# Hybrid attention and mixture-of-experts layer: the attention output is summed inside TensorE's back transposes and scaled by VectorE, and TensorE multiplies during its waits for the routing tables

## The chip, the cores and the metric

The kernel runs on one core of one Trainium2 chip. The metric is the device time of one execution in microseconds (us); less is better. The core's engines work side by side and wait for each other by semaphores: TensorE (PE, with its weight loads PEld), VectorE (DVE), ScalarE (ACT), GpSimd (POOL) and SyncE (SP, which issues most transfers).

## The reference

One layer on 1024 tokens plus 16 meta tokens, model width 1024, float32, batch 1:

```
h = h + hybrid_mixer(rmsnorm(h))   # two attention branches of 8 heads each, gated, one output projection
h = h + hier_moe(rmsnorm(h))       # top-1 of 4 groups, then top-2 of its 8 experts; 32 experts of width 256
out = rmsnorm(h)[:, 16:]

# attention, both branches, head width 64 (v) and chunk-causal mask:
p = softmax(s);  o = einsum('bhqk,bkhd->bqhd', p, v)
```

In branch A (dense heads) s is q times k with a rotary part; in branch B (sparse heads) only the 256 best keys of an indexer take part, with a bias by relative position. The experts' input rows are gathered by tables that are computed on the chip: for each token its two experts, its rank in each expert's list, and from these the slot of each token.

## The kernel before

One program goes through stages that are separated by blocks: input projection and indexer, threshold search, low-rank projections, attention, branch and output projections with the router, routing tables, 32 experts, final norm.

**Attention.** There are 16 heads, first 8 dense, then 8 sparse (HH = 16), and two super-steps s for each: an even (short) one over query blocks 0 to 3 with 5 key tiles, and an odd (long) one over query blocks 4, 5, 7, 6 with 9 key tiles. A super-step's softmax is computed per query block: TensorE makes the scores (`qk`), VectorE the row maximum (`row_max`; in sparse heads the score step that adds the bias and finds the maximum), ScalarE the exponential and its sum `den`; VectorE's reciprocal of `den` is `rec`. The order on TensorE is a list of turns, written out when the program is built. A "p" turn transposes one key tile of the probabilities (up to four 128x128 blocks) into a PSUM bank; ScalarE copies it as the rounded `pH`, VectorE writes the remainder `pL`, and three turns later TensorE multiplies both with the values (`pv`). Three PSUM banks rotate among the turns; `emptied(k)` is the wait until the reader of an earlier turn on the same bank is done. Because the values are split too (`VS` holds the rounded value in 64 columns and the remainder in the next 64), the output of a super-step is 128 rows for 64 channels: rows c and 64 + c have to be added.

For this there is one "q" turn per super-step, 32 in all. It is inserted at place 5 of the next super-step's turns, after ScalarE's copy `oT` of the output (L1329). TensorE transposes the four query blocks back to tokens (L1268), VectorE adds the two halves (`tensor_reduce` into `otmp`, L1389), and GpSimd multiplies by `rec` into `otok` (L1402, function `scaled`). Two heads share `otok`; an "o" turn, for every second head, transposes it (L1270), and ScalarE copies it to `OaT` or `ObT` (L1333). GpSimd's queue holds, per super-step, the split of the next head's values, queries and keys, then `scaled` of the super-step before, and at odd ones the issue of a bias join for a later head.

TensorE's operands are of two kinds: a tile declared F32R is multiplied in one pass as it is; the large products are therefore made of three such products of leading parts and remainders. Tiles declared F32 (as `ident`, `con`, `oT`, the router's `x2T` and `wr`) are multiplied as true fp32. `pe.transpose` uses the transpose mode.

**Around the branch projections.** After attention a block ends, semaphores are cleared, and the next block starts. There ScalarE (`rows_lead`) and VectorE (`rows_rest`) split the attention outputs, and TensorE's first product (L1578) waits for the first remainder.

**Routing tables** (`moe_tables`). VectorE runs a long chain of small steps. TensorE's part is `ranks`: it waits for `both` (s_rk), makes ranks (L1931, L1933) and totals (L1937), waits for the operands A and B (s_ab) and makes the slot products (L1942), waits again (s_ab) and makes the slots' weights (L1946). The slots give the tokens, by which GpSimd gathers the first expert's rows; then TensorE transposes them (L2238) and goes on with the experts.

Of the kernel before, what the change touches and what calls it, by code (L numbers as in the profile page):

```python
# [14 lines left out]
ALU = mybir.AluOpType  # L15
# [7 lines left out]
P = 128  # L23
# [65 lines left out]
def hybrid_layer(nc, a, out):  # L89

    ctx = ExitStack()
    with ctx:
# [63 lines left out]
        dmaskb = keep("dmaskb", 64, BF16)  # L156
        upperb = keep("upperb", P, BF16)
        onesb = keep("onesb", P, BF16)
        gcq = keep("gcq", 2)
        gckv = keep("gckv", 1)  # L160
        nhalf = keep("nhalf", 18)
# [194 lines left out]
        with block() as blk:  # L356
# [512 lines left out]
            def _(dve):  # L869
# [39 lines left out]
                dve.tensor_copy(dmaskb[:, :], con[:, K_DM:K_DM + 64]).then_inc(s_cb, 1)  # L909
                dve.tensor_copy(upperb[:, :], con[:, K_U:K_U + P]).then_inc(s_cb, 1)  # L910
                dve.memset(onesb[:, :], 1.0).then_inc(s_cb, 1)
                for n, (kind, p, t, part) in enumerate(idx_jobs):
                    bank = ps[:, 4 + n % 4, :]
                    dve.wait_ge(s_ie, 2 * (n + 1))
                    if kind == "q":
                        for u in range(2):
                            c, j = slice(512 * part, 512 * (part + 1)), 4 * p + 2 * t + u
                            lead = Qi2[64 * u:64 * (u + 1), j, c].bitcast(F32)
                            dve.tensor_tensor(Qi2[64 * (1 - u):64 * (2 - u), j, c],
                                              bank[64 * u:64 * (u + 1), :], lead, ALU.subtract).then_inc(s_il, 1)  # L920
                    else:
                        lo, hi = thirds[part]
                        for u in range(2):
                            dve.tensor_tensor(KiLo[64 * u:64 * (u + 1), lo:hi], bank[0:64, 0:hi - lo],
                                              KiHi[0:64, lo:hi].bitcast(F32), ALU.subtract).then_inc(s_il, 1)
# [121 lines left out]
        pH = [at(f"pH{k}", [P, 512], F32R, R_X + 4096 * k) for k in range(RING)]  # L1047
        pL = [at(f"pL{k}", [P, 512], F32R, R_X + 4096 * k + 2048) for k in range(RING)]
        oT = [at(f"oT{k}", [P, 512], F32, R_X + 4096 * RING + 2048 * k) for k in range(2)]
        otmp = [at(f"otmp{k}", [P, 4, VD], F32, R_S + 16384 + 1024 * k) for k in range(2)]  # L1050
        OaT = at("OaT", [P, 4, T], F32, R_W)
        ObT = at("ObT", [P, 4, T], F32, R_S)
        KR = [at(f"KR{k}", [P, L], F32, R_K + 4160 * k) for k in range(2)]
# [87 lines left out]
        def bank_of(k):  # L1141
            return ps[:, bank_no[k], :]

        (s_qk, s_ml, s_ex, s_t, s_ld, s_rs, s_pv, s_ot, s_qa, s_rc, s_om, s_oe, s_z, s_vz, s_hl, s_hr, s_vl,
         s_vr) = map(sem, ["s_qk", "s_ml", "s_ex", "s_t", "s_ld", "s_rs", "s_pv", "s_ot", "s_qa", "s_rc",
                           "s_om", "s_oe", "s_z", "s_vz", "s_hs", "s_hr", "s_vl", "s_vr"])

        with block() as blk:
# [51 lines left out]
            def _(pe):  # L1200
# [35 lines left out]
                def emptied(k):  # L1236
                    kind, s, _ = turns[k]
                    if kind == "p":
                        pe.wait_ge(s_rs, p_no[turns[k]] + 1)
                    elif kind == "q":  # L1240
                        pe.wait_ge(s_qa, s + 1)
                    else:
                        pe.wait_ge(s_oe, o_no[turns[k]] + 1)

                def turn(k):
# [17 lines left out]
                    for b in range(low(s, t) // P if kind == "p" else 0, 4):  # L1263
                        dst = bank[:, P * b:P * (b + 1)]
                        if kind == "p":
                            mm = pe.transpose(dst, px(s, 4 * (s % 2) + b)[:, P * t:P * (t + 1)], ident)  # L1266
                        elif kind == "q":
                            mm = pe.transpose(dst, oT[s % 2][:, P * b:P * (b + 1)], ident)  # L1268
                        else:
                            mm = pe.transpose(dst, otok[s % 2][:, P * b:P * (b + 1)], ident)  # L1270
                    mm.then_inc(s_t, 1)
# [66 lines left out]
            def _(dve):  # L1338
# [30 lines left out]
                for k in range(len(turns)):  # L1369
# [3 lines left out]
                    if kind == "p":  # L1373
                        if t == 0:
                            dve.wait_ge(s_ex, 4 * s + 4)
                            c = 4 * (s % 4)
                            if s >= 4:
                                dve.wait_ge(s_om, s - 3)
                            dve.reciprocal(rec[:, c:c + 4], den[:, c:c + 4]).then_inc(s_rc, 1)
                        n, lo = p_no[turns[k]], low(s, t)  # L1380
                        dve.wait_ge(s_ld, n + 1)
                        dve.tensor_tensor(pL[n % RING][:, lo:512], bank_of(k)[:, lo:512],  # L1382
                                          pH[n % RING][:, lo:512].bitcast(F32), ALU.subtract).then_inc(s_rs, 1)
                    elif kind == "q":
                        dve.wait_ge(s_t, k + 1)
                        if s >= 2:
                            dve.wait_ge(s_om, s - 1)
                        both = bank_of(k).rearrange("p (b l c) -> p b c l", b=4, l=2)
                        dve.tensor_reduce(otmp[s % 2][:, :, :], both, AX.X, ALU.add).then_inc(s_qa, 1)  # L1389
                    if k in qk_after and not opens(k):  # L1390
                        row_max(qk_after[k])

            @blk.gpsimd
            def _(pool):
                def scaled(s):
                    u, c = s // 2 % 2, 4 * (s % 4)
                    pool.wait_ge(s_qa, s + 1)
                    pool.wait_ge(s_rc, s + 1)
                    if s >= 4:
                        before = ("o", 4 * (s // 4) - 4 + 2 + s % 2, 0)  # L1400
                        pool.wait_ge(s_t, turn_of[before] + 1)
                    pool.tensor_tensor(otok[s % 2][:, :].rearrange("p (b c) -> p b c", b=4)[:, :, VD * u:VD * (u + 1)],  # L1402
                                       otmp[s % 2][:, :, :],
                                       rec[:, c:c + 4].unsqueeze(2).to_broadcast([P, 4, VD]),
                                       ALU.mult).then_inc(s_om, 1)

                def values(hh):
                    if hh >= 2:
                        pool.wait_ge(s_pv, p_no[last_tile(2 * (hh - 2) + 1)] + 1)
# [46 lines left out]
                for s in range(NSS):  # L1456
# [6 lines left out]
                            queries(hh + 1)  # L1463
                    elif hh + 1 < HH:
                        keys(hh + 1)
                    if s >= 1:
                        scaled(s - 1)
                    if s % 2 == 1 and s // 2 + 2 < H:
                        joined(pool, s // 2 + 2)
                scaled(NSS - 1)  # L1470

        with block() as blk:
            @blk.gpsimd
# [51 lines left out]
        with block() as blk:  # L1525
# [36 lines left out]
                        sp.dma_start(xn2_d[P * (b - 1):P * b, :], x2[(b - 1) % 2][:, :]).then_inc(s_xos[(b - 1) % 2], 16)  # L1562
            @blk.tensor
            def _(pe):
                for n in range(JOBS):
                    m, part = n // 2, n % 2
                    pe.wait_ge(s_bl, m + 1)
# [258 lines left out]
def moe_tables(nc, a, at, sem, block, ps, con, rl, upperb, onesb, R_H, R_K, wts, xn2_d, s_xos):  # L1826
# [88 lines left out]
    def gathers(pool):  # L1915
# [6 lines left out]
        for u in range(U):  # L1922
            pool.indirect_dma_start(out=xs[u][:, :], out_offset=None, in_=xn2_d,
                                    in_offset=bass.IndirectOffsetOnAxis(ap=tok_i[:, u:u + 1], axis=0),
                                    bounds_check=T - 1, oob_is_err=False).then_inc(wts["G"][u], 16)

    def ranks(pe):
        pe.wait_ge(s_rk, 1)
        for b in range(NB):
            for c in range(b):  # L1930
# [5 lines left out]
        for b in range(NB):  # L1936
            mm = pe.matmul(ps[:, 1, 0:NE], onesb[:, :], both[:, b, :], start=(b == 0), stop=(b == NB - 1))  # L1937
        mm.then_inc(s_rk, 1)
        for n in range(N2):
            if n % PART == 0:  # L1940
                pe.wait_ge(s_ab, 2 + n // PART)
            mm = pe.matmul(ps[:, 2, 0:NE], A[:, n, :], B[:, n, :], start=(n == 0), stop=(n == N2 - 1))  # L1942
        mm.then_inc(s_sl, 1)
        pe.wait_ge(s_ab, 2 + N2 // PART)
        for n in range(N2):
            mm = pe.matmul(ps[:, 3, 0:2 * NE], A[:, n, :], BW[:, n, :, :].rearrange("p c n -> p (c n)"),  # L1946
# [708 lines left out]
```

## Time and profile before

| | |
|---|---|
| median of 3 runs | 1461.71 us (1460.07 to 1461.95) |
| the profiled execution's own time | 1460.28 us |
| its span, first to last instruction | 1458.5 us |
| busy: PE / DVE / ACT / POOL | 1361.1 / 1007.6 / 659.6 / 459.2 us |
| attention stage | about 536 to 847 us |
| branch, output projections and router | 849 to 1054 us |
| routing tables (first transfer issue to first expert's transposes) | 1054.3 to 1077.9 us |

The profile is of one execution. A line of a timeline gives the start, the length, engine, line, what is written and read, the count of merged records, and in square brackets how long the engine was idle before it and what ended that. The lengths of matmul records overlap, since they are pipelined: what one costs TensorE is the distance from its start to the next one's start. PEclk is the share of TensorE's 2.4 GHz that was granted; 0.50 is its lower level, 1.2 GHz. A wait for several semaphores is put down to the one that came last by the profile.

### The profile page before, as it was taken

The page shows a single profiled execution, that of the slowest core. Times are in us where ns is not written, and L with a number is a line of the kernel's source. Part 1 is how long each engine was busy: PE and PEld are TensorE (multiplying, and loading weights), DVE is VectorE, ACT ScalarE, POOL GpSimd, SP SyncE. Part 2 cuts the span into 40 slices and gives each one's busy share as a digit, 9 for nine tenths or more (in the row PEclk, how much of TensorE's full clock was granted, in tenths as well). Part 3 has the DMA queues.
Part 4 walks back from the last instruction along what each step waited for, and adds up shares of the span by engine and source line. Part 5 has one row for each costly group of instructions (what it writes and reads, how often), then busy time and mean ns, then how long its engine had stood idle before and what let it go on. Part 6 is the DMA issues. An engine that isn't in the chain of part 4 may idle for free. (4 is left out here: it accounts for less than half of the span.)

```text
span 1458.5 us, 21714 instructions
## 1 busy us (share of the span) xinstructions
PE 1361.1 (93%) x7307; PEld 1117.2 (77%) x7308; DVE 1007.6 (69%) x1891; ACT 659.6 (45%) x1175; POOL 459.2 (31%) x497
## 2 busy tenths in 40 slices
PE   6989999999999999999999979999859999999973
PEld 4779888888989978888777768899857776777741
DVE  5448999999970277777777754342387777777746
ACT  5348323321212146777777741121135666666622
POOL 1100335421215545555555214200112332333313
PEclk9999999999999999999999989999959999999996
DMA  6031543257432904868776255222279999999818
GB/s 213 30 143 40 185 161 111 88 197 228 134 101 100 246 1 80 187 134 225 210 206 179 68 178 159 86 89 87 73 281 389 348 366 351 356 379 372 344 58 326
DMA packets 106926, 273.76 MB, mean 188 GB/s; under 512 B 27393, under 2 KB 56737, under 8 KB 94425
## 3 DMA queue, kind: packets, MB, share of 16 engines
q1 hardware_dynamic: 92208, 229.20, 45.5%
q0 software_dynamic: 13584, 38.62, 10.4%
q10 hardware_dynamic: 1048, 4.82, 0.9%
q8 instruction: 52, 0.85, 0.2%
q14 instruction: 34, 0.27, 0.1%
HBM read 246.99 MB, written 85.96 MB: 228 GB/s over the span
## 5 line engine op out<-in xcount | busy, mean ns | idle before, releaser
L445 PE MATMUL ps<-hHi,g_lead 128*128 128x512 f32 (+2 forms) x480 | 184.5, 384 | 5.8 <-DVE hLo L877 3.6
L330 DVE TENSOR_SCALAR_CACHE_REDUCE mask<-score,cand 128x272 bf16<-128x272 f32 (+6 forms) x224 | 185.5, 892 | 4.6 <-DVE cand L349 4.4
L2364 DVE TENSOR_TENSOR w_rest<-wgu,w_lead 128x1024 fp32r<-128x1024 f32 x128 | 156.0, 1222 | 46.4 <-ACT w_lead L2309 45.2
L446 PE MATMUL ps<-hLo,g_lead 128*128 128x512 f32 (+2 forms) x480 | 183.9, 383 | 0.0
L447 PE MATMUL ps<-hHi,g_rest 128*128 128x512 f32 (+2 forms) x480 | 182.6, 380 | 0.0
L1382 DVE TENSOR_TENSOR pL<-ps,pH 128x512 fp32r<-128x512 f32 (+3 forms) x224 | 124.8, 573 | 56.8 <-ACT pH L1321 54.2
L2309 ACT CAST w_lead<-wgu 128x1024 fp32r<-128x1024 f32 x124 | 130.8, 1055 | 48.3 <-PE ps L2252 48.3
L762 POOL TENSOR_TENSOR g_rest<-g_raw,g_lead 128x2048 fp32r<-128x2048 f32 x12 | 56.7, 4722 | 298.4 <-ACT g_lead L619 298.4
L1321 ACT CAST pH<-ps 128x512 fp32r<-128x512 f32 (+3 forms) x224 | 106.0, 495 | 53.8 <-PE ps L1266 53.1
L2250 PE MATMUL ps<-w_lead,x_lead 128*128 128x512 f32 x256 | 114.5, 447 | 4.0 <-DVE x_rest L2371 4.0
L2272 PE MATMUL ps<-wd,hmT 128*128 128x512 f32 x256 | 115.3, 593 | 1.6 <-DVE hmT L2387 1.0
L445 PEld LDWEIGHTS ps<-hHi,g_lead 128*128 128x128 f32 x480 | 90.9, 189 | 22.8 <-ACT relf L701 4.0
L447 PEld LDWEIGHTS ps<-hHi,g_rest 128*128 128x128 f32 x480 | 91.0, 190 | 16.7
L446 PEld LDWEIGHTS ps<-hLo,g_lead 128*128 128x128 f32 x480 | 90.8, 189 | 14.8
L2252 PE MATMUL ps<-w_lead,x_rest 128*128 128x512 f32 x256 | 102.0, 398 | 0.0
L2251 PE MATMUL ps<-w_rest,x_lead 128*128 128x512 f32 x256 | 101.1, 395 | 0.0
L2214 POOL DMA_INDIRECT ys_d<-ye,dk x32 | 32.2, 1007 | 216.5 <-DVE ye L2399 180.3
L1282 PE MATMUL ps<-pH,VS 128*128 128x512 f32 (+3 forms) x224 | 94.9, 424 | 0.9
L2272 PEld LDWEIGHTS ps<-wd,hmT 128*128 128x128 f32 x256 | 46.2, 190 | 47.8 <-issue 47.8
L1283 PE MATMUL ps<-pL,VS 128*128 128x512 f32 (+3 forms) x224 | 79.0, 353 | 0.0
L650 ACT ACTIVATE stage<-ps 128x512 f32<-128x512 f32 x32 | 19.1, 598 | 112.1 <-PE ps L447 112.0
L2250 PEld LDWEIGHTS ps<-w_lead,x_lead 128*128 128x128 f32 x256 | 49.2, 192 | 20.9 <-issue 7.2
(382 smaller groups left out, 3414.3 us busy)
## 6 DMA issues: line engine op xcount, KB each, us to landing
wgu<-in_w_exp_gate SPq DMA_DIRECT2D x32, 1024.0 KB
wgu<-in_w_exp_up SPq DMA_DIRECT2D x32, 1024.0 KB
wd<-in_w_exp_down SPq DMA_DIRECT2D x32, 1024.0 KB, 11.8
bias_d<-mask_d POOLq DMA_DIRECT2D x8, 2368.0 KB, 15.6
g_raw<-in_w_in SPq DMA_DIRECT2D x16, 1024.0 KB, 7.2
gates_d<-stage SPq DMA_DIRECT2D x32, 256.0 KB, 2.0
gt<-gates_d SPq DMA_DIRECT2D x32, 256.0 KB, 3.1
tbm<-bias_d SPq DMA_DIRECT2D x8, 976.0 KB, 6.2
```

The lines of the kernel that those rows point to most:

```text
L330: return dve.tensor_scalar(mask[:, OFF[i]:OFF[i + 1]], score[:, OFF[i]:OFF[i + 1]], thr, 0.0, op, ALU.add, accum_out=cnt[:, i:i + 1])
L445: pe.matmul(dst, x[0], y[0], start=(k == 0), stop=False)
L446: pe.matmul(dst, x[0], y[1], start=False, stop=False)
L447: return pe.matmul(dst, x[1], y[0], start=False, stop=(k == KT - 1))
L1321: act.copy(pH[n % RING][:, lo:512], bank_of(k)[:, lo:512]).then_inc(s_ld, 1)
L1382: dve.tensor_tensor(pL[n % RING][:, lo:512], bank_of(k)[:, lo:512], pH[n % RING][:, lo:512].bitcast(F32), ALU.subtract).then_inc(s_rs, 1)
L2250: pe.matmul(dst, xl[:, k, :], wl, start=(k == 0), stop=False)
L2251: pe.matmul(dst, xl[:, k, :], wr, start=False, stop=False)
L2252: mm = pe.matmul(dst, xr[:, k, :], wl, start=False, stop=(k == KT - 1))
L2272: mm = pe.matmul(ps[:, 5 + half, :], hmT[u % 2][:, k, :], wd[u][:, k, 512 * half:512 * (half + 1)], start=(k == 0), stop=(k == 1))
L2309: act.copy(w_lead[part][:, :, :, :], wgu[u][:, :, 2 * part:2 * part + 2, :]).then_inc(S["m_wl"], 1)
L2364: dve.tensor_tensor(w_rest[u][:, :, 2 * part:2 * part + 2, :], wgu[u][:, :, 2 * part:2 * part + 2, :], w_lead[part][:, :, :, :].bitcast(F3 ...
```

## The change

In attention the q turn no longer transposes with the identity. TensorE multiplies the same `oT` block with `fold`, a 128x64 tile of two identity matrices one above the other, which adds the halves while it transposes; the result has 64 columns per query block instead of 128. VectorE no longer reduces, it multiplies the four 64-column blocks by `rec` straight from PSUM into `otok`. GpSimd's `scaled`, the tile `otmp` and the semaphore s_qa are gone; the bank of a q turn is free when s_om has counted VectorE's multiplication. `fold` is built once by VectorE beside the other constants.

TensorE also gets fp32 products of a 128x128 with a 128x512 operand whose results are never read: two at the start of the block of the branch projections, three before its wait for `both` in the tables, two after the totals and one after the slot products.

```
+        fold = keep("fold", VD)
...
+                dve.tensor_tensor(fold[:, :], ident[:, 0:VD], ident[:, VD:2 * VD], ALU.add).then_inc(s_cb, 1)
...
-        otmp = [at(f"otmp{k}", [P, 4, VD], F32, R_S + 16384 + 1024 * k) for k in range(2)]
...
                     elif kind == "q":
-                        pe.wait_ge(s_qa, s + 1)
+                        pe.wait_ge(s_om, s + 1)
...
                         elif kind == "q":
-                            mm = pe.transpose(dst, oT[s % 2][:, P * b:P * (b + 1)], ident)
+                            mm = pe.matmul(bank[:, VD * b:VD * (b + 1)], oT[s % 2][:, P * b:P * (b + 1)], fold[:, :],
+                                           start=True, stop=True)
...
                     elif kind == "q":
                         dve.wait_ge(s_t, k + 1)
-                        if s >= 2:
-                            dve.wait_ge(s_om, s - 1)
-                        both = bank_of(k).rearrange("p (b l c) -> p b c l", b=4, l=2)
-                        dve.tensor_reduce(otmp[s % 2][:, :, :], both, AX.X, ALU.add).then_inc(s_qa, 1)
+                        dve.wait_ge(s_rc, s + 1)
+                        if s >= 4:
+                            dve.wait_ge(s_t, turn_of[("o", 4 * (s // 4) - 4 + 2 + s % 2, 0)] + 1)
+                        u, c = s // 2 % 2, 4 * (s % 4)
+                        dve.tensor_tensor(otok[s % 2][:, :].rearrange("p (b c) -> p b c", b=4)[:, :, VD * u:VD * (u + 1)],
+                                          bank_of(k)[:, 0:4 * VD].rearrange("p (b c) -> p b c", b=4),
+                                          rec[:, c:c + 4].unsqueeze(2).to_broadcast([P, 4, VD]),
+                                          ALU.mult).then_inc(s_om, 1)
...
-                def scaled(s):
-                    u, c = s // 2 % 2, 4 * (s % 4)
-                    pool.wait_ge(s_qa, s + 1)
-                    pool.wait_ge(s_rc, s + 1)
-                    if s >= 4:
-                        before = ("o", 4 * (s // 4) - 4 + 2 + s % 2, 0)
-                        pool.wait_ge(s_t, turn_of[before] + 1)
-                    pool.tensor_tensor(otok[s % 2][:, :].rearrange("p (b c) -> p b c", b=4)[:, :, VD * u:VD * (u + 1)],
-                                       otmp[s % 2][:, :, :],
-                                       rec[:, c:c + 4].unsqueeze(2).to_broadcast([P, 4, VD]),
-                                       ALU.mult).then_inc(s_om, 1)
...
             def _(pe):
+                for _ in range(2):
+                    pe.matmul(ps[:, 7, :], ident, con[:, 0:512], start=True, stop=True)
...
+    def awake(pe, turns):
+
+        for _ in range(turns):
+            pe.matmul(ps[:, 5, :], con[:, K_ID:K_ID + P], con[:, 0:512], start=True, stop=True)
+
     def ranks(pe):
+        awake(pe, 3)
         pe.wait_ge(s_rk, 1)
...
         mm.then_inc(s_rk, 1)
+        awake(pe, 2)
         for n in range(N2):
...
         mm.then_inc(s_sl, 1)
+        awake(pe, 1)
         pe.wait_ge(s_ab, 2 + N2 // PART)
```

## Rows read from the trace of the kernel before

**Rows 1.** Busy time (count) per engine, PEclk, DMA: dense head, sparse head, experts.
```profile
655.90:675.40 19.50, 19.20 (x138) 16.57 (x137) 14.20 (x27) 14.01 (x33) 11.15 (x12) 1.00 0.74 143
749.60:767.80 18.20, 17.11 (x113) 14.28 (x112) 14.90 (x36) 13.86 (x33) 10.29 (x11) 1.00 0.71 204
1110.00:1410.00 300.00, 298.44 (x1243) 211.83 (x1242) 228.85 (x326) 181.28 (x233) 91.52 (x114) 1.00 0.89 334
```

**Rows 2.** Timeline, dense head: row maximum after the reduction of a q turn.
```profile
656.87 0.71 DVE L1363 TENSOR_REDUCE negm<-ps 128x1 f32<-128x528 f32 x1 [0.24 <-PE ps L1233]
```

**Rows 3.** Timeline, sparse head: around a short and a long super-step's q turn.
```profile
742.89 0.33 PE L1266 MATMUL ps<-con,px 128*128 128x128 f32 x1 [0.59 <-DVE pL L1382]
...
749.57 0.68 DVE L1389 TENSOR_REDUCE otmp<-ps 128x256 f32<-128x512 f32 x1
...
750.90 0.74 ACT L1308 ACTIVATE px<-sbias,negm 128x528 f32<-128x528 f32 x1 [0.36 <-DVE negm L1359]
```

**Rows 4.** Timeline of TensorE, dense head: the two q turns and what follows.
```profile
654.99 0.60 PE L1268 MATMUL ps<-con,oT 128*128 128x128 f32 x4
655.35 0.48 PE L1282 MATMUL ps<-pH,VS 128*128 128x512 f32 x1
...
668.87 0.34 PE L1283 MATMUL ps<-pL,VS 128*128 128x384 f32 x1
669.32 0.65 PE L1266 MATMUL ps<-con,pxa 128*128 128x128 f32 x4
```

**Rows 5.** Timeline of TensorE, router: fp32 products of 36 columns.
```profile
1006.94 1.87 PE L1602 MATMUL ps<-wr,x2T 128*128 128x36 f32 x16
1008.65 0.47 PE L1617 MATMUL ps<-wo_lead,y_lead 128*128 128x512 f32 x1
```

**Rows 6.** Timeline of TensorE, final stage: fp32 products of 512 columns.
```profile
1426.72 2.07 PE L2590 MATMUL ps<-fa,con 128*128 128x512 f32 x2 [13.15 <-DMA fb<-ys_d]
1428.58 1.91 PE L2591 MATMUL ps<-fb,con 128*128 128x512 f32 x2
```

**Rows 7.** Groups by form, attention stage: reduction, its multiplication, a 256-column remainder.
```profile
L1389 DVE TENSOR_REDUCE otmp<-ps 128x256 f32<-128x512 f32 x32 | 21.9, 683 | 2.8 <-PE ps L1268 2.6
L1402 POOL TENSOR_TENSOR otok<-otmp,rec 128x256 f32<-128x256 f32 x32 | 19.6, 613 | 140.3 <-DVE otmp L1389 139.6
...
L1382 DVE TENSOR_TENSOR pL<-ps,pH 128x256 fp32r<-128x256 f32 x32 | 13.3, 417 | 0.5
```

**Rows 8.** Busy time and granted clock (PEclk) where it is low or rises.
```profile
539.80:546.40 6.60, 6.57 (x25) 5.95 (x26) 2.82 (x5) 2.75 (x7) 6.44 (x6) 0.50 0.00 0
852.60:857.00 4.40, 4.36 (x10) 3.47 (x11) 4.40 (x5) 4.40 (x6) 0.00 (x0) 0.50 0.85 255
857.00:861.00 4.00, 4.00 (x19) 3.24 (x18) 4.00 (x5) 1.64 (x2) 0.00 (x0) 1.00 1.05 401
1061.50:1067.70 6.20, 1.34 (x45) 1.23 (x45) 5.93 (x19) 4.21 (x6) 0.00 (x0) 0.50 1.00 423
1067.70:1085.60 17.90, 13.55 (x50) 12.01 (x51) 12.75 (x31) 2.21 (x3) 6.15 (x7) 0.50 0.61 226
1426.70:1430.50 3.80, 3.78 (x5) 1.72 (x6) 1.23 (x1) 0.72 (x2) 0.76 (x2) 0.50 1.02 417
```

**Rows 9.** Timeline, end of attention and start of the branch projections.
```profile
843.99 0.66 PE L1268 MATMUL ps<-con,oT 128*128 128x128 f32 x4 [0.21 <-ACT oT L1329]
...
845.46 0.61 POOL L1402 TENSOR_TENSOR otok<-otmp,rec 128x256 f32<-128x256 f32 x1 [4.38 <-DVE otmp L1389]
...
846.12 0.66 PE L1270 MATMUL ps<-con,otok 128*128 128x128 f32 x4 [1.47 <-POOL otok L1402]
...
852.64 0.77 PE L1578 MATMUL ps<-o_lead,wb_lead 128*128 128x512 f32 x1 [5.87 <-DVE o_rest L1696]
```

**Rows 10.** Timeline of TensorE, routing tables: slot products, weight products.
```profile
1067.70 3.60 PE L1942 MATMUL ps<-r_B,r_A 128*128 128x32 f32 x16 [4.86 <-DVE r_A L2060]
1074.25 1.06 PE L1946 MATMUL ps<-r_BW,r_A 128*128 128x64 f32 x4 [2.95 <-DVE r_BW L2083]
```

More of the change, by code:

```diff
@@ L1142, in bank_of @@
             return ps[:, bank_no[k], :]
-        (s_qk, s_ml, s_ex, s_t, s_ld, s_rs, s_pv, s_ot, s_qa, s_rc, s_om, s_oe, s_z, s_vz, s_hl, s_hr, s_vl,
-         s_vr) = map(sem, ["s_qk", "s_ml", "s_ex", "s_t", "s_ld", "s_rs", "s_pv", "s_ot", "s_qa", "s_rc",
+        (s_qk, s_ml, s_ex, s_t, s_ld, s_rs, s_pv, s_ot, s_rc, s_om, s_oe, s_z, s_vz, s_hl, s_hr, s_vl,
+         s_vr) = map(sem, ["s_qk", "s_ml", "s_ex", "s_t", "s_ld", "s_rs", "s_pv", "s_ot", "s_rc",
                            "s_om", "s_oe", "s_z", "s_vz", "s_hs", "s_hr", "s_vl", "s_vr"])
@@ L1465, in _ @@
                         keys(hh + 1)
-                    if s >= 1:
-                        scaled(s - 1)
                     if s % 2 == 1 and s // 2 + 2 < H:
                         joined(pool, s // 2 + 2)
-                scaled(NSS - 1)
         with block() as blk:
```

## The prediction

> **What bounds the kernel now.** I read the page first, then busy time by stage, the groups by form in the attention stage, TensorE's timeline in one head of either kind, the two places where its clock is low, and last the waits around the turn that changes. In both kinds of head TensorE is the fullest engine, but not equally [rows 1]: a dense head (two super-steps, 19.5 us) has it busy 19.20 us, a sparse head (18.2 us) 17.11 us, and there VectorE is busy 14.90 us. In the expert stage it is busy 298.44 of 300 us. So whatever the stages before the experts lose or win comes out at the end: nothing later waits for anything else.
>
> In a dense head TensorE goes from one product to the next with almost no gap, and after the turn of the change VectorE waits for TensorE: the row maximum that follows the reduction starts 0.24 us after it could, "<-PE" [rows 2]. In a sparse head it is mixed: TensorE waits 0.59 us for VectorE's remainder in the short super-step [rows 3], and in the long one ScalarE waits 0.36 us for VectorE's score step.
>
> **What a q turn costs TensorE.** There are 32 q turns. Before, one is 4 transposes of 128x128 in transpose mode, one record each. They start at 654.99 and the next product at 655.35 [rows 4]: 0.36 us, 0.09 each. After, it is 4 true fp32 products with 64 moving columns. The trace has no such product with 64 columns; the nearest is the router's fp32 product with 36 columns. Its 8 products of one block leave 16 records, so each is issued as two instructions, each with a weight load; they start at 1006.94 and the next line at 1008.65 [rows 5]: 1.71 us, 0.107 per instruction. A 64-column stream is shorter than that at full clock (each instruction of a 512-column fp32 product starts 0.93 us after the one before at half clock [rows 6], so 64 columns are about 0.12 at half and 0.06 at full), so the load sets the pace and 0.107 holds. The new turn is 8 x 0.107 = 0.86 us, and the difference +0.49 us. Bounds: if the pair cost one load, 4 x 0.107 = 0.43, so +0.07; above, 0.49 in every turn.
>
> By the Trainium skill, FP8 and Floating Point Precision, section TensorE Precision Notes, true FP32 takes 4 passes through the array; 4 x 64 columns at 2.4 GHz are 0.107 us a product, 0.43 us a turn and only 0.07 us more than before, if the passes alone set the price. The rows above, where 36 columns cost 0.21 us a product, speak against reading it so: by the rows it is 0.86.
>
> **What a q turn costs VectorE.** The reduction from 512 PSUM columns takes 683 ns; a VectorE product over 128x256 with one PSUM operand takes 417 ns [rows 7]. I take 417 for the multiplication by rec: 0.27 us less a turn, 32 x 0.27 = 8.5 us of VectorE. GpSimd loses 32 x 613 ns, and with them its waits for VectorE (139.6 us) [rows 7]. Behind that wait stood the values, the keys and the bias join of later heads; they start earlier. Nobody on the other engines waits for them by any long row, so I price this at 0. The new waits of VectorE are for rec, which its own queue wrote a super-step before, and for an o turn of the super-step before: both long done. The bank of a q turn is freed 0.49 - 0.27 = 0.22 us later; the three banks rotate, so the turn that needs it comes three turns later, and this is hidden. One more VectorE instruction of 64 columns builds fold, long before attention; it is under the 417 ns of the 256-column one, 0 where TensorE's projections cover it.
>
> **What of it comes out, turn by turn.**
> Dense, long super-step, 8 turns: TensorE runs on without a gap after 655.35, and VectorE waits for it. All of the 0.49 comes out and none of VectorE's 0.27: +3.9.
>
> Dense, short super-step, 7 turns: after the turn TensorE streams a 384-column product from 668.87 (0.17 us: 384 of 512 columns of the 0.21 to 0.23 us that a product of 512 takes at full clock [rows 8]) and then idles 0.28 until 669.32, when ScalarE's exponential is ready [rows 4]. That exponential does not wait for the q turn. 0.28 is absorbed, 0.21 comes out: +1.5.
>
> Sparse, short super-step, 8 turns: the gap before 742.89 [rows 3] swallows it: 0.
>
> Sparse, long super-step, 8 turns: VectorE reduces from 749.57 and then does the score step, for which the exponential at 750.90 waits 0.36 us. VectorE's saving brings the score step up to 0.27 forward; TensorE's 0.49 pushes back both the product that it reads and the next transposes, whose copy ScalarE must make before that exponential. The two nearly cancel. I take +0.1 a turn: +0.8. Bounds: VectorE's chain alone decides, 8 x -0.27 = -2.1; or TensorE's cost in all 16 sparse turns, 16 x 0.49 = +7.8.
>
> The tail, 1 turn: the whole chain is exposed. From the last q turn (843.99) to the last o turn (846.12) [rows 9] lie the turn, the reduction and GpSimd's multiplication, which with its hand-over takes 845.46 to 846.12 = 0.66. New: +0.49 - 0.27 - 0.66 = -0.4.
>
> Attention: 3.9 + 1.5 + 0 + 0.8 - 0.4 = +5.8 us.
>
> **The products nobody reads, before the branch projections.** TensorE idles 5.87 us before 852.64 [rows 9], and when it starts its granted clock is 0.50, the 1.2 GHz level; it is at 2.4 GHz from 857.0, after 4.4 us of uninterrupted products [rows 8]. Those 4.4 us hold 10 products, 0.44 us each, the next 4.0 us 19, 0.21 each. So a microsecond at the low clock loses about half of itself, here 2.2 us. The two new products are fp32 with 512 columns, two instructions each, 0.93 us an instruction at 1.2 GHz [rows 6]: 3.7 us. They can start when the block does; from the end of the last o turn, 846.12 + 0.6, a block's change takes some 2.3 us, so at about 849.05, and they end at 852.8, 0.1 us late. If the clock again rises 4.4 us after the first product, that is 853.5: 0.7 us of low clock remain, 0.4 us. The gain is 2.2 - 0.4 - 0.1 = 1.7; I take 1.6. Bounds: two other starts of this trace stayed low for 3.8 and 6.6 us of work [rows 8], which gives 2.0 and 0.6; with no earlier rise, -0.1. VectorE's remainders come every 1.2 us for 1.4 us of full-clock products, so they can follow.
>
> **Those around the tables.** Three before the choice: 5.6 us at 1.2 GHz, from 1054.3, so over before the ranks start at 1061.5. Two after the totals, behind 1.34 us of rank products from 1061.5 [rows 8]: 3.7 us, over at 1066.6, 1.1 us before the slot products may start at 1067.70. One after those (1071.3): 1.9 us, over at 1073.2, before 1074.25 [rows 10]. So they delay nothing; cover left is 1.0 us and more. They pay if the clock is up at 1067.70: 16 products in 3.60 us, the clock 0.50 all through to 1085.6 [rows 8, 10]. At full clock the slot products end when their last operand allows, about 1.4 us sooner. But the fill before them lasts 3.7 us, 5.1 with the rank products, close to the 4.4 after which the clock rose elsewhere, and 1.1 us of idleness follows. I take 0.4 (1 in 3 of 1.2). Bounds: 0, and 5 if the full clock lasts into the first expert (1.4, then 1.8 of the weight products, and 2.0 of the ten wide products at low clock before 1085.6).
>
> **Sum.** +5.8 - 1.6 - 0.4 = +3.8 us. The profiled execution has a span of 1458.5 and a time of 1460.28; with the change 1464.1. The median of the runs shown is 1461.71, 1.4 above it, so the forecast is 1465.5, +0.26%.
>
> **Rivals.**
> 1. The fold products cost TensorE as little as the transposes, and VectorE's relief decides (faster). Then the dense turns give 15 x 0.07 = 1.0 or less, the long sparse ones -2.1, the tail 0.07 - 0.27 - 0.66 = -0.9, the fillers -2.0: 1461.7 - 4.0 = 1457.7. For it: VectorE's 82% in sparse heads. Against it: two records, each with a load, for a product in [rows 5]. It decides where TensorE's turn stays under 0.5 us. 0.2. (The rule of the Trainium skill weighed above, in FP8 and Floating Point Precision, would have it so.)
> 2. The clock stays up through the tables (same): the forecast with 5 instead of 0.4, 1460.9. Against it: fill and gap alternate. 0.1.
> 3. TensorE's cost comes out in every turn: 31 x 0.49 - 0.4 - 2.0 = +12.8, or 1474.5; half as far, 1470. For it: 94% busy in the sparse head. Against it: the waits in [rows 3]. 0.12.
> 4. The fillers do nothing, because the clock rises no sooner: +5.8, 1467.5. 0.1.
> The forecast, 1462.5 to 1469: 0.48.
>
> A measurement of this kernel can tell about 0.2% (2.9 us) from no change: faster is under 1458.8, slower over 1464.6. Faster is 0.17 of rival 1 and 0.03 of rival 2; same their rest, 0.10, and the low end of the forecast, 0.18; the rest is slower, 0.52. The range is 1457.5 to 1470.
>
> **What would show it.** In the profile after: eight records of the fold product a turn, 0.107 us apart; the distance from one q turn to the next but one 19.5 to about 20.2 us in dense heads and about 18.3 in sparse ones; VectorE's multiplication at about 420 ns; the clock up near 853 plus the shift; no new wait in the tables. I am wrong if the records are four, if dense heads keep 19.5 us, or if the clock is at 1.0 during the slot products.

## The result

| | median | lowest to highest | runs |
|---|---|---|---|
| before | 1461.21 us | 1459.78 to 1462.50 | 20 |
| after | 1463.91 us | 1461.53 to 1465.73 | 20 |

The ratio is 1.0018 [1.0012, 1.0024]: 2.7 us slower, with an interval of about 1.8 to 3.5 us. The forecast was 1465.5, or +3.8 us, with a range of 1457.5 to 1470. The profiled execution of after has a span of 1460.9 us and a time of 1462.73, against 1458.5 and 1460.28; the forecast for that execution was 1464.1.

### The profile page after: what moved, and what is told of

The parts are those of the page before. It is cut to its first block and busy times, and to the rows that moved or that the text cites. A ratio compares the mean times of both kernels' runs of the same rounds, so it can differ in the third digit from the quotient of the medians.

```text
span 1460.9 us, 21941 instructions
## 1 busy us (share of the span) xinstructions
PE 1381.9 (95%) x7451; PEld 1134.9 (78%) x7452; DVE 1001.9 (69%) x1892; ACT 659.7 (45%) x1175; POOL 441.4 (30%) x465
## 6 DMA issues: line engine op xcount, KB each, us to landing
bias_d<-mask_d POOLq DMA_DIRECT2D x8, 2368.0 KB, 15.6
```

## The profile after

The first page view, the busy time of each engine over the span:

```profile
span 1460.9 us, 21941 instructions
...
PE 1381.9 (95%) x7451; PEld 1134.9 (78%) x7452; DVE 1001.9 (69%) x1892; ACT 659.7 (45%) x1175; POOL 441.4 (30%) x465
```

TensorE is 21 us busier, VectorE 6 and GpSimd 18 us less. These sums say what moved, not what it cost: the time grew by 2.7 us only.

**The q turn.** First the source line of the fold product with all its instructions (shortest, median and longest record in ns), and who waited for it; then two groups by form in the attention stage (busy us, mean ns, then the idle time before them):

```profile
L1269 PEld LDWEIGHTS ps<-fold,oT x256: 186/192/193, 557.6 to 850.2; 128*128 128x128 f32 x128
L1269 PE MATMUL ps<-fold,oT x256: 217/275/323, 557.9 to 850.3; 128*128 128x64 f32 x128
...
  DVE otok L1392: 6.7, 12
```

```profile
L1384 DVE TENSOR_TENSOR pL<-ps,pH 128x256 fp32r<-128x256 f32 x32 | 13.3, 417 | 0.5
...
L1392 DVE TENSOR_TENSOR otok<-ps,rec 128x256 f32<-128x256 f32 x32 | 13.5, 421 | 6.7 <-PE ps L1269 6.7
```

There are 256 records for 128 products (32 turns of four), each record with its own weight load. VectorE's multiplication lasts 421 ns. Against [rows 7] the reduction and GpSimd's multiplication are gone, and VectorE now waits 6.7 us for TensorE where it waited 2.6.

TensorE's timeline in a dense head, around its two q turns:

```profile
657.98 1.00 PE L1269 MATMUL ps<-fold,oT 128*128 128x64 f32 x8
658.78 0.48 PE L1284 MATMUL ps<-pH,VS 128*128 128x512 f32 x1
...
671.58 1.00 PE L1269 MATMUL ps<-fold,oT 128*128 128x64 f32 x8
672.41 0.28 PE L1267 MATMUL ps<-con,px 128*128 128x128 f32 x1
672.45 0.42 PE L1284 MATMUL ps<-pH,VS 128*128 128x384 f32 x1
672.71 0.33 PE L1285 MATMUL ps<-pL,VS 128*128 128x384 f32 x1
672.88 0.60 PE L1267 MATMUL ps<-con,pxa 128*128 128x128 f32 x4
673.23 0.36 PE L1284 MATMUL ps<-pH,VS 128*128 128x256 f32 x1
```

Read the distance from each start to the next line's start. The turn in the long super-step takes 0.80 us, where [rows 4] have 0.36. In the short super-step it is 0.83, and before, the same four transposes took from 668.15 to 668.58, 0.43. The 384-column product is followed after 0.17 us by the next transposes, where [rows 4] have 0.45: the exponential is ready by then, so the 0.28 us of waiting are gone. The four transposes behind it take 0.35 us instead of 0.41 (before 669.32 to 669.73).

This is one of two kinds of short super-step. In the other kind (four of the seven of the dense heads) the wait was longer. Before:

```profile
570.81 0.34 PE L1283 MATMUL ps<-pL,VS 128*128 128x384 f32 x1
571.33 0.66 PE L1266 MATMUL ps<-con,pxa 128*128 128x128 f32 x4 [0.18 <-ACT pxa L1308]
571.75 0.36 PE L1282 MATMUL ps<-pH,VS 128*128 128x256 f32 x1
```

and after:

```profile
572.13 0.34 PE L1285 MATMUL ps<-pL,VS 128*128 128x384 f32 x1
572.30 0.60 PE L1267 MATMUL ps<-con,pxa 128*128 128x128 f32 x4
572.66 0.36 PE L1284 MATMUL ps<-pH,VS 128*128 128x256 f32 x1
```

From the 384-column product to the transposes it was 0.52 us and is 0.17, so 0.35 of waiting are gone, and the transposes take 0.36 instead of 0.42.

Busy time, clock and traffic of a dense head, a sparse head and the experts, as in [rows 1]; here each window is about one head long:

```profile
658.90:678.93 20.03, 19.84 (x144) 17.50 (x144) 13.79 (x26) 14.13 (x33) 9.38 (x9) 1.00 0.85 208
754.10:772.40 18.30, 17.90 (x122) 15.47 (x121) 14.74 (x37) 13.86 (x33) 9.18 (x8) 1.00 0.69 205
1111.20:1411.20 300.00, 298.44 (x1243) 211.82 (x1242) 228.84 (x326) 181.33 (x233) 92.37 (x114) 1.00 0.88 334
```

The dense head grew with TensorE's work. In the sparse head TensorE is busy 17.90 us instead of 17.11 in almost the same time: there most of the new work went into its waits. In the expert stage TensorE is as busy as before, 298.44 us.

The end of attention and the start of the branch projections, TensorE's timeline (compare [rows 9]), and the clock there:

```profile
849.42 1.10 PE L1269 MATMUL ps<-fold,oT 128*128 128x64 f32 x8 [0.21 <-ACT oT L1331]
851.04 0.66 PE L1272 MATMUL ps<-con,otok 128*128 128x128 f32 x4 [0.52 <-DVE otok L1392]
853.99 3.65 PE L1557 MATMUL ps<-con 128*128 128x512 f32 x4 [2.29 <-PEq L106]
857.55 0.47 PE L1571 MATMUL ps<-o_lead,wb_lead 128*128 128x512 f32 x1
857.85 0.40 PE L1572 MATMUL ps<-o_rest,wb_lead 128*128 128x512 f32 x1
```

```profile
854.10:857.50 3.40, 3.40 (x4) 0.93 (x4) 2.46 (x3) 3.40 (x4) 0.00 (x0) 0.50 0.58 180
857.50:861.00 3.50, 3.50 (x16) 2.92 (x16) 3.50 (x4) 3.50 (x5) 0.00 (x0) 1.00 0.87 288
```

From the last q turn to the last o turn it is 1.62 us, before 2.13. The unread products lie wholly inside the wait: the first real product starts 6.51 us after the last o turn, before 6.52. And it starts at the full clock; in [rows 8] the first ten products ran at 0.50. How many real products run slowly differs from trace to trace, though: six to thirteen in the five traces of this case without these two unread products, and none to five in the four traces with them. From the first branch product to the first output projection the five take 89.2 (before), 88.6, 88.6, 88.9 and 89.8 us, the four 87.1 (after), 87.1, 87.8 and 88.3.

The routing tables, TensorE's timeline and the clock of two stretches (compare [rows 10] and [rows 8]):

```profile
1065.52 3.76 PE L1923 MATMUL ps<-con 128*128 128x512 f32 x4
1070.55 2.68 PE L1942 MATMUL ps<-r_B,r_A 128*128 128x32 f32 x16 [1.27 <-DVE r_A L2061]
1073.08 2.05 PE L1923 MATMUL ps<-con 128*128 128x512 f32 x2
1076.18 3.62 PE L1947 MATMUL ps<-r_BW,r_A 128*128 128x64 f32 x16 [1.06 <-DVE r_BW L2084]
```

```profile
1070.50:1072.60 2.10, 2.05 (x14) 1.81 (x15) 2.06 (x6) 0.00 (x0) 0.00 (x0) 0.99 1.03 433
1072.60:1086.20 13.60, 11.14 (x37) 8.49 (x37) 9.54 (x23) 1.22 (x3) 6.14 (x7) 0.50 0.56 194
```

The slot products ran at the full clock and took 2.68 us instead of 3.60; then it fell, and the weight products took 3.62 us at the low level, as before. TensorE was free 1.27 and 1.06 us before either, so the fillers (the unread products) delayed nothing.

**Where the 2.4 us of span went.** By the starts of the same instruction in both traces, the shift grows and shrinks so: first scores +0.3 (535.8 to 536.1); first sparse head's first q turn +4.3 (705.30 to 709.56); last q turn +5.4; last o turn +4.9; first branch product +4.9; first output projection +2.8 (941.9 to 944.7); rank products +2.8; first expert's transposes +1.9; its first down projection +1.3; the last one +1.3; first product of the final norm +2.0; span +2.4.

## The experiments

Each kernel is compared with runs of the kernel before on its own chip. The median of these was 1461.25 us (21 runs) for the first two kernels below, 1462.51 (10 runs, another chip) for the kernel with the fold only in the last turn, and 1461.23 (29 runs) for the other four. Differences in us are worked out from the medians or, with their bounds, from the ratios.

### All the unread products on the kernel before

```
+                for _ in range(2):
+                    pe.matmul(ps[:, 7, :], ident, con[:, 0:512], start=True, stop=True)
...
+        awake(pe, 3)
...
+        awake(pe, 2)
...
+        awake(pe, 1)
```

> The kernel before with all the unread products and nothing else. My theory expects the opposite share: 2.1 us in the branch projections and about 1 us around the tables, so -2 to -3 us, ratio 0.998 to 0.9985. The rival (they do nothing, the phases of the clock alone differ) expects no difference.

Measured: 1458.44 (11 runs), ratio 0.9981 [0.9972, 0.9990], so 2.8 us faster (1.5 to 4.1). TensorE's timeline where the branch projections start:

```profile
848.92 3.75 PE L1566 MATMUL ps<-con 128*128 128x512 f32 x4 [2.31 <-PEq L106]
852.48 0.77 PE L1580 MATMUL ps<-o_lead,wb_lead 128*128 128x512 f32 x1
853.04 0.63 PE L1581 MATMUL ps<-o_rest,wb_lead 128*128 128x512 f32 x1
853.47 0.63 PE L1582 MATMUL ps<-o_lead,wb_rest 128*128 128x512 f32 x1
```

Here the clock came up only at 854.9, after five and a half real products, and the stage from its first product to the first output projection takes 88.3 us, against 89.2 before and 87.1 after. So in single executions these fillers brought 0.9 and 2.1 us against this one trace of before; over all nine traces the means of this stage are 87.6 us with them and 89.0 without, 1.4 apart. The tables show no gain in this execution (16.6 us from the ranks to the first expert's transposes, before 16.4). In time, the unread products as a whole are worth 2.8 us here, and 1.5 between the fold alone (below) and the change; the forecast's 2.0 lies between.

### Only those around the tables

The diff is the one above without its first two lines.

> The kernel before with only the six unread products around the routing tables. In the changed kernel the last slot product came 0.85 us nearer to the ranks than before, because the clock had risen a little before the slot products. My theory, that this depends on where the rise falls, expects -0.5 to -1 us, ratio 0.9995, more spread than the others. The rival, that the tables gain nothing since the weight products after them are at the low clock again, expects 0.

Measured: 1460.47 (11 runs), 0.9998 [0.9989, 1.0007]: no difference that can be told, as the rival had it. The slot products took 3.3 us up to the weights' filler and the ranks-to-transposes stretch 16.3 us, as before (16.4). On the same chip the two branch products thus make the difference between 1460.47 and 1458.44, 2.0 us; the eleven times of the one lie between 1459.49 and 1462.19, of the other between 1456.86 and 1459.86.

### The fold without any unread product

```
-                for _ in range(2):
-                    pe.matmul(ps[:, 7, :], ident, con[:, 0:512], start=True, stop=True)
...
-        awake(pe, 3)
...
-        awake(pe, 2)
...
-        awake(pe, 1)
```

(taken from the kernel after)

> The attention part of the change alone, none of the unread products. My theory (TensorE's eight instructions a q turn come out in the dense heads, the unread products give part of it back) expects attention 4.5 to 5 us longer and all of it at the end: about +4.9 us, ratio 1.0034. The rival, that the later stages absorb part of a shift in attention and the unread products do nothing, expects +2.7 us as in the changed kernel, ratio 1.0018.

Measured: 1465.40 (7 runs), 1.0028 [1.0017, 1.0039], so 4.2 us slower (2.5 to 5.7). The rival's +2.7 lies inside these bounds; what speaks against it is that the unread products alone do give time (above). From the first q turn to the last it is 291.67 us, in after 291.54, before 286.52. The attention part of the change is the loss; the fillers take part of it back.

### VectorE's part alone

Transposes are kept; VectorE multiplies the leading 64 columns of each transposed block by `rec` and the remainders' columns are left out of the output. No unread products.

```
-                            mm = pe.matmul(bank[:, VD * b:VD * (b + 1)], oT[s % 2][:, P * b:P * (b + 1)], fold[:, :],
-                                           start=True, stop=True)
+                            mm = pe.transpose(dst, oT[s % 2][:, P * b:P * (b + 1)], ident)
...
-                                          bank_of(k)[:, 0:4 * VD].rearrange("p (b c) -> p b c", b=4),
+                                          bank_of(k).rearrange("p (b c) -> p b c", b=4)[:, :, 0:VD],
```

> TensorE as before (four transposes a turn); VectorE multiplies the leading halves by rec straight from PSUM, and the remainders' halves are left out of the output; GpSimd's multiplication is gone. This is what the shorter VectorE instruction alone is worth. My working expects -0.9 us in the tail, between 0 and -2.1 us in the long super-steps of the sparse heads and nothing in the dense heads: -1 to -3 us. If VectorE bounded attention, 32 x 0.27 = -8.5 us.

Measured: 1458.47 (11 runs), 0.9981 [0.9972, 0.9990]. The group of its multiplication, with the wait before it:

```profile
L1391 DVE TENSOR_TENSOR otok<-ps,rec 128x256 f32<-128x256 f32 x32 | 13.4, 417 | 2.8 <-PE ps L1269 2.6
```

Six dense heads take 117.39 us (before 117.40): the relief is worth nothing there. Seven sparse heads take 126.32 (before 127.99), 0.24 us a head less, and the tail from the last q turn to the last o turn 1.18 instead of 2.13. That is 2.6 us in the trace, with the stretch between dense and sparse heads (12.11 to 11.88) 2.85, and 2.8 timed. This kernel differs from the fold without unread products only in which instructions TensorE issues for the turn, and in the columns that VectorE reads: the eight instructions in place of four cost 291.67 - 284.62 = 7.05 us from first to last q turn, and 1465.40 - 1458.47 = 6.9 us in the times.

### The fold as a one-pass product

`oT` and `fold` are declared F32R, so the attention output is rounded to its leading part before the product. No unread products.

```
-        fold = keep("fold", VD)
+        fold = keep("fold", VD, F32R)
...
-        oT = [at(f"oT{k}", [P, 512], F32, R_X + 4096 * RING + 2048 * k) for k in range(2)]
+        oT = [at(f"oT{k}", [P, 512], F32R, R_X + 4096 * RING + 2048 * k) for k in range(2)]
```

> As the fold alone, but oT and fold are declared F32R, so that a product is one instruction with one load; the attention output is rounded to its leading part on the way. If the number of TensorE instructions sets the loss (my theory), four of them cost 0.43 us a turn against the transposes' 0.36: the dense heads lose 0.1 us or less each, and with the tail (-1 us) the kernel is within 1 us of the one before. If instead VectorE's new instruction or the changed order of GpSimd's work were the cause, the loss of about 5 us stays.

Measured: 1458.89 (11 runs), 0.9982 [0.9973, 0.9991]: 2.3 us faster than before, where I had expected it within 1 us; I had left out what VectorE's part alone brings in the sparse heads. Its group, and the same turn of a dense head in TensorE's timeline:

```profile
L1269 PE MATMUL ps<-fold,oT 128*128 128x64 f32 x128 | 17.0, 256 | 0.2 <-ACT oT L1331 0.2
```

```profile
655.76 0.53 PE L1269 MATMUL ps<-fold,oT 128*128 128x64 f32 x4
656.12 0.48 PE L1284 MATMUL ps<-pH,VS 128*128 128x512 f32 x1
```

128 records instead of 256, and a turn of 0.36 us, as with the transposes of [rows 4]. Dense heads take 117.50 us for six, sparse ones 126.32 for seven, the same as with VectorE's part alone. So the loss comes with the true fp32 product, which is issued as two instructions with a load each, and not with VectorE's new multiplication or GpSimd's changed order, which are the same here. Loads and passes were not taken apart by a run of their own; but an instruction costs 0.107 us with 36 columns [rows 5] and 0.10 with 64 (0.80 for eight), so the columns do not set the price.

### All the unread products, and the fold only in the last turn

On the kernel before: all the unread products, and the fold product and VectorE's multiplication for the last super-step alone, where nothing covers the chain.

```
+                        elif kind == "q" and s == NSS - 1:
+                            mm = pe.matmul(bank[:, VD * b:VD * (b + 1)], oT[s % 2][:, P * b:P * (b + 1)], fold[:, :],
+                                           start=True, stop=True)
```

> A version that keeps what paid: the kernel before with all the unread products, and the fold only in the last q turn, where the chain is exposed. My theory expects the gain of the unread products alone and 0.5 us more: -2.5 to -3.5 us, ratio 0.998. If the fold is no loss in itself, it is no better than the unread products alone.

Measured: 1458.23 (6 runs), 0.9968 [0.9956, 0.9980] against its chip's own 1462.51. The tail:

```profile
844.22 1.10 PE L1270 MATMUL ps<-fold,oT 128*128 128x64 f32 x8 [0.21 <-ACT oT L1334]
845.84 0.65 PE L1275 MATMUL ps<-con,otok 128*128 128x128 f32 x4 [0.52 <-DVE otok L1396]
```

1.62 us, as in after and 0.51 less than before. This is the fastest kernel by its ratio (the medians are 4.3 us apart, more than the 2.5 to 3.5 expected, with only six runs). Its interval overlaps that of the fillers alone, so the 0.5 us is read from the trace and not from the times.

### The same with more unread products around the tables

```
-        awake(pe, 2)
+        awake(pe, 3)
...
-        awake(pe, 1)
+        awake(pe, 2)
```

> As the kernel before with all the unread products and the fold in the last q turn only, but with three instead of two unread products between totals and slot products, and two instead of one after those. If the clock is what the slot and weight products lack, it is up through them and into the first expert: 1 to 4 us less than with two and one. If the added products only come late, they delay the slot products: at the low clock three take 5.6 us where 5.3 are free, +0.3 to +0.5 us, and two 3.7 us where 3.3 are free, +0.4 us.

Measured: 1458.00 (11 runs), 0.9978 [0.9969, 0.9987]. TensorE's timeline in the tables, and the clock in the slot products and at the start of the first expert:

```profile
1061.40 4.99 PE L1947 MATMUL ps<-con 128*128 128x512 f32 x6
1066.44 2.43 PE L1966 MATMUL ps<-r_B,r_A 128*128 128x32 f32 x16
1068.71 3.31 PE L1947 MATMUL ps<-con 128*128 128x512 f32 x4
1071.81 2.33 PE L1971 MATMUL ps<-r_BW,r_A 128*128 128x64 f32 x16
1075.54 1.67 PE L2263 MATMUL ps<-con,xs 128*128 128x128 f32 x8 [1.39 <-DMA xs<-xn_d,tok_i]
1078.61 0.79 PE L2275 MATMUL ps<-w_lead,x_lead 128*128 128x512 f32 x1 [1.40 <-DVE x_rest L2396]
```

```profile
1066.40:1068.60 2.20, 2.16 (x16) 1.92 (x16) 2.13 (x7) 0.00 (x0) 0.00 (x0) 1.00 1.06 447
1076.00:1082.80 6.80, 5.40 (x17) 4.12 (x16) 5.35 (x11) 2.21 (x3) 1.91 (x4) 0.50 0.72 248
```

Now both table products are fast (2.43 and 2.33 us). Yet the stretch from the ranks to the first expert's transposes is 15.3 us. With fewer fillers it was 15.4 (after) and 15.6 (fold in the last turn), but 16.6 and 16.3 in the two kernels with nothing but fillers, and 16.4 before; the clock was up at the slot products only in the first two (0.99 and 0.85, against 0.50 and 0.54). What limits the stretch here: VectorE's last operand, ready at about 1068.1, ends the slot products (the last starts at 1068.6), and the gather of the rows ends the wait after the weights. The clock, still at 1.00 after that wait, is at 0.50 from 1076.0 on, so the expert's first wide products are slow as before. The times of this kernel, 1458.00, and of the fillers alone, 1458.44, cannot be told apart: the 1 to 4 us that were expected of a clock that stays up did not come.

### Five kernels that ran empty

In five kernels the `@` in front of each engine's function was missing, so the engines had no program and the time was 4.5 us; they tell nothing of any theory. The first was meant to be the fold without unread products (measured above):

> The attention part of the change alone, none of the unread products. My theory (TensorE's eight instructions a q turn come out in the dense heads, the unread products give part of it back) expects attention 4.5 to 5 us longer and all of it at the end: about +4.9 us, ratio 1.0034. The rival, that the later stages absorb part of a shift in attention and the unread products do nothing, expects +2.7 us as in the changed kernel, ratio 1.0018.

The unread products ahead of the branch projections alone; this was not measured, and their worth is taken from the difference of the two filler kernels:

> The kernel before with only the two unread products ahead of the branch projections. If they raise the clock before the first real product, the projections start at full clock: -1.5 to -2.1 us, ratio 0.9988. If the low clock is only moved, 0.

The one-pass fold (measured above):

> As the fold alone, but oT and fold are declared F32R, so that a product is one instruction with one load; the attention output is rounded to the leading part on its way. If the number of TensorE instructions sets the loss (my theory), four of them cost 0.43 us a turn against the transposes' 0.36: the dense heads lose 0.1 us or less each, and with the tail the kernel is at -0.5 us, within 1 us of the one before. If instead VectorE's new instruction or the later start of the o turns were the cause, the loss of about 5 us stays.

VectorE's part alone (measured above):

> TensorE as before (four transposes a turn); VectorE multiplies the leading halves by rec straight from PSUM and the remainders' halves are left out of the output; GpSimd's multiplication is gone. This is what the shorter VectorE instruction alone is worth. My working expects -0.9 us in the tail and between 0 and -2.1 us in the long super-steps of the sparse heads, nothing in the dense heads: -1 to -3 us. If VectorE bounded attention, 32 x 0.27 = -8.5 us.

More unread products around the tables (measured above):

> As the version that keeps what paid, with three instead of two unread products between totals and slot products, and two instead of one after those. If the clock is what the slot and weight products lack, it is up through them and the first expert: 1.5 to 4 us less than that version. If the added products only come late, they delay the slot products: at the low clock three take 5.6 us where 5.3 are free, +0.3 to +0.5 us, and two 3.7 us where 3.3 are free, +0.4 us.

## Why the prediction was right

The direction, the place and the mechanism held: TensorE's eight instructions cost time where it is the bound, and VectorE, the tail and the fillers give back less than that. The size was too large: +3.8 us were forecast and +2.7 measured, which is also in the band of 1458.8 to 1464.6 that I had given 0.28, while I had given 0.52 to more. In the times, the attention part alone is +4.2 (forecast +5.8) and the fillers on top of it -1.5 (forecast -2.0). Point by point, from the traces:

- **The turn's price.** Forecast 8 x 0.107 = 0.86, so +0.49. Shown: 0.80 us in a long super-step, so +0.44; in the short ones 0.81 against 0.36, +0.45, or 0.83 against 0.43, +0.40. Two instructions a product, each with a load, as [rows 5] had it. The reading of the Trainium skill (FP8 and Floating Point Precision, TensorE Precision Notes) by which four passes of 64 columns alone set the price would have made it 0.43, an estimate from its figure; the trace, with 0.80, does not agree.
- **Dense, long.** From one q turn to the next 13.16 us became 13.61 (576.73 to 589.89, and 577.64 to 591.25): +0.45. Seven are like this; the eighth, which runs on into the first sparse head, goes from 12.11 to 12.36, +0.25. Together +3.4, forecast +3.9.
- **Dense, short.** Forecast +0.21 a turn; the next q turn comes after 6.58 instead of 6.54 us (from 570.19 and 571.06): +0.04, and in the kind at 668.15 after 6.35 instead of 6.26: +0.09. This is the term that was mis-sized most: +0.5 us for seven turns, forecast +1.5. In the second kind +0.40 for the turn, -0.28 for the exponential's wait as forecast, and -0.06 because the transposes that no longer stand behind a wait go faster leave +0.06, and 0.03 more come by the next q turn. In the first kind the wait that covers the turn was 0.35 us: +0.45 - 0.35 - 0.06 = +0.04. I had taken the gap of one turn for all seven, and the turn's price 0.04 to 0.09 too high. Both kinds together, to the first sparse head: 147.83 us became 151.68, +3.9, forecast +5.4. A dense head, from one q turn to the next but one, is now 19.95 us (before 19.42), where about 20.2 was named as the sign.
- **Sparse, short.** Forecast 0. The intervals 6.70 and 5.92 us are the same in both traces.
- **Sparse, long.** Forecast +0.1 as a near balance of two unknowns. The heads alternate: 12.11 stays 12.11, 11.67 becomes 11.92. With VectorE's part alone they are 11.87 and 11.46, so VectorE's relief is worth 0.21 to 0.24 (the bound was 0.27) and TensorE's turn costs 0.24 in one kind and 0.46, nearly all of it, in the other. Of the eight turns four add nothing, three add 0.24 us each, and the last, after which no further head follows, adds 0.44 (5.25 to 5.69). Over the stage, 138.69 us became 139.86: +1.2, forecast +0.8.
- **The tail.** Forecast -0.4, shown -0.5 (2.13 to 1.62).
- **Attention in all.** Forecast +5.8, shown +4.6 up to the last o turn (4.9 less the 0.3 that the trace was late before attention began).
- **Branch fillers.** Forecast -1.6; -2.1 in this trace, -0.9 in the trace with the fillers alone, -1.4 between the means of the nine traces, and -2.0 between the medians of the two kernels that differ in them. The size held on average; where the clock rises in one execution is luck. No delay, where 0.1 was forecast.
- **Table fillers.** Forecast -0.4; -0.9 in this trace. I had written that the clock at 1.0 during the slot products would show me wrong, and it was at 0.99. That sign was a wrong one, and the term came near by luck: I had taken 1.2 us at 1 in 3, and about 0.9 came in three traces of five with these fillers. What kept the sum right is what came after: it fell again before the weight products, and the 4 to 5 us of rival 2, which needed it through the first expert, did not appear. The times of these fillers alone show no difference (bounds -1.6 and +1.0 us).

The sum of the trace is +4.6 - 2.1 - 0.9 = +1.6, and with the 0.3 at the start +1.9. The rest of the span's +2.4 lies after the tables: -0.6 in the first expert, where the granted clock is 0.51 for 3.5 us (1096.4 to 1099.9) and before 0.50 for 6.8 (1092.6 to 1099.4), and +0.8 before the final norm, where TensorE waits for the transfer of `fb` 13.9 us instead of 13.15, and +0.4 in the last stage. These were not tested and may be scatter between executions.

Rival 1, the fold as cheap as the transposes, is what the one-pass kernel made real: 1458.89 without fillers, where the rival's terms without fillers gave 1461.7 - 2.0 = 1459.7. It does not hold for the true fp32 product. Rival 3 fell: seven sparse heads grew by 0.7 us, where it had 14 x 0.49 = 6.9. Rival 4 fell: fillers on the kernel before give 0.9981. Rival 2 did not come either, as said under the table fillers.

Not tried: the one-pass fold with the unread products, which should be faster than either alone by the terms above (an estimate), at the price of a rounded attention output; and fillers that reach through the gather into the first expert.

## What to carry to other kernels

Before replacing a transpose by a product that also does arithmetic, look up how many records, each with a weight load, such a product leaves in the trace. For a few columns their number is its price (here 0.10 us each), and it is paid in full where TensorE has no wait to cover it, while the vector work saved there is worth nothing. An edit that appears once per loop turn can be right in the one exposed turn (here the last: -0.5 us) and wrong in the others; it can be made there alone. Products that nobody reads gave about 2 us ahead of a long dense stretch, where they fit the wait, and nothing that could be told between short steps, where another operand or a transfer ends the wait anyway.

## What the hardware showed that I had not expected

- A q turn of four one-pass products, whose loads last 190 ns each in the records, takes 0.36 us, just as one of four transposes, whose loads last 140 ns (the kernels with the one-pass fold and with VectorE's part alone). The length of a load's record is not its price; the distance between starts is.
- The same unread products before the same stage ended in full clock at once in one trace (first real product at 857.55 and the clock at 1.00 from 857.5) and 2.4 us later in another (first real product 852.48, clock up at 854.9), with the same 3.5 us of unread work before it. Without unread products it differed as much: in the kernel before ten real products ran slowly, with the one-pass fold thirteen, with only the table fillers six. What one execution gains is not what the next gains, so a filler is judged by times and not by one trace.
